# The first products of an encoder kernel issued one by one as their operands come, with the first statistics behind both groups

## The chip, the cores and the metric

One core of a Trainium2 chip runs the whole program. The metric is device time in microseconds, the median of the runs of one kernel. TensorE multiplies, VectorE and ScalarE do arithmetic and copies, GpSimd (POOL in the profile) a few additions and its own DMAs, and SyncE (SP) issues most of the DMAs.

## The reference

Two layers over 512 tokens of width 1024, in float32. Each layer is a token mixer and a squared-ReLU MLP with 4096 hidden units, each ahead of it an RMS norm and behind it a plain residual addition; a last RMS norm ends it.

```python
def rms_norm(x, g):
    y = xf * lax.rsqrt(jnp.mean(xf * xf, axis=-1, keepdims=True) + EPS)
    return (y * g.astype(jnp.float32)).astype(x.dtype)

def reference(...):
    for i in range(DEPTH):
        h = rms_norm(x, mix_norm[i])
        if i % N_MIXERS == 0:
            x = x + neighbourhood_attention(h, na_w_qkv[j], na_rpb[j], na_w_o[j])
        else:
            x = x + sliding_window_gqa(h, swa_w_qkv[j], swa_sinks[j], t5_rel_table, swa_w_o[j])
        h = rms_norm(x, mlp_norm[i])
        x = x + squared_relu_mlp(h, mlp_w_in[i], mlp_w_out[i])
    return rms_norm(x, final_norm)
```

The change lies in the first norm of layer 0 and the first three groups of its QKV projection: queries, keys and values of the first pair of heads.

## The kernel before

**Layout.** x is held transposed: 8 tiles (k = 0 to 7) of 128 features by 512 tokens. Weights come in a stream of chunks of 128x1024 (8 blocks of 128x128), through the two halves of `w_raw`. A group n is one output tile of 128x512, the sum over the 8 tiles k.

**Split precision.** Every operand is cut into a high part (a copy rounded to fp32r) and a low part (what the rounding left). A product of two operands is three matmuls, high by high, high weights by low h, low weights by high h; `part` (L654 to L656 by way of `product`) issues the three of each tile k in a row. ScalarE makes the high parts, VectorE the low ones. A chunk's high part is counted by the semaphore `w_hi_made`, its low part by `w_split`; for h the counters are `first_hi` and `h_low`.

**The norm.** h here is x times the gain, without the division by the root of the mean square, which is applied to the products at the end. ScalarE squares each tile (L1457), VectorE adds the squares into `sqsum` (`first_sum`, L1611, counter `h_split`). TensorE sums over the partitions, one column for 128 tokens (`token_statistics`, L729); ScalarE takes the root (L1124), VectorE the reciprocal (L1972), TensorE spreads the four columns back over the partitions (`spread_token_rstd`, L737), ScalarE copies them to `rstd` (L1127), and VectorE scales the groups' sums with it (`scale_tile`, L1531).

**Around the change.** Each engine runs its own list in the written order; semaphores alone tie them together. At the start TensorE runs 12 matmuls on constant data (`keep_busy`, L723), then `first_groups`: for each k, behind `h_low` k+1, the three matmuls of group 0 and, from k = 1, those of group 1 (tile 0 of group 1 between); the statistics stand ahead of group 1's last tile, the spread behind it, and then all of group 2, whose weights (the third chunk) lie in a spare place and whose sums have a bank of their own (`first_values`). Then comes `na_step(1)`, whose scores (L774) need queries and keys scaled and split (`tile_high` L1145 on ScalarE, `tile_low` L1541 on VectorE, counter `tile_split`). VectorE's list at the start is: split of chunk 0, low parts of h 0 and 1, split of chunk 1, low part 2, additions 0 and 1, then in turn a low part and an addition; behind them, the split of the third chunk (L1616), the reciprocal, scaling of groups 0 and 1, the split of the fourth chunk, the two `tile_low`, the scaling of group 2. ScalarE waits for addition k − 3 before its square k, as three squares fit in the buffer. GpSimd adds the mask to the attention bias (L563) and issues its DMAs (L552). SyncE loads a chunk when the chunk before the last has been split.

Of the kernel before, what the change touches and what calls it, by code (L numbers as in the profile page):

```python
# [22 lines left out]
P = 128  # L23
# [5 lines left out]
KT = D // P  # L29
# [132 lines left out]
def encoder(nc, xT, wstream, gains, rpb, sinks, rel_table, na_mask, onehot, out):  # L162
# [4 lines left out]
    with ExitStack() as ctx:  # L167
        def sb(name, shape, dt=F32):
            return ctx.enter_context(nc.sbuf_tensor(name, shape, dt))

        def sem(name):
            return ctx.enter_context(nc.semaphore(name))

        x = sb("x_res", [P, KT, SEQ])
        h_hi, h_lo = sb("h_hi", [P, KT, SEQ], F32R), sb("h_lo", [P, KT, SEQ], F32R)
# [6 lines left out]
        def chunk_parts(t, half):  # L182
            return w_parts[:, half, t, 0:2 * CHUNK].rearrange("p (n f) -> p n f", n=2)

        w_hi, w_lo = chunk_parts(0, 0), chunk_parts(1, 0)
# [48 lines left out]
        acc = [ctx.enter_context(nc.psum_tensor(f"acc{n}", [P, SEQ], F32)) for n in range(2)]  # L234
# [18 lines left out]
        w_hi_made, w_split, w_used = sem("w_hi_made"), sem("w_split"), sem("w_used")  # L253
# [14 lines left out]
        idle_made, h_low, first_hi = sem("idle_made"), sem("h_low"), sem("first_hi")  # L268
# [24 lines left out]
        spare_hi, spare_lo = (t[:, 0:2, :].rearrange("p a b -> p (a b)") for t in (u_hi, u_lo))  # L293
        first_values = pt_ps[:, 4:8, :].rearrange("p a b -> p (a b)")

        def f32(ap):
            return ap.bitcast(F32)
# [57 lines left out]
        def first_square(k):  # L355

            return probs[:, SEQ * (k % 3):SEQ * (k % 3 + 1)]
# [293 lines left out]
        def _(pe):  # L651
            def product(dst, a, b, start, stop, resumed=False):

                nc.tensor.matmul(dst, a[0], b[0], start=start, stop=False, skip_group_check=resumed)  # L654
                nc.tensor.matmul(dst, a[0], b[1], start=False, stop=False, skip_group_check=resumed)  # L655
                return nc.tensor.matmul(dst, a[1], b[0], start=False, stop=stop, skip_group_check=resumed)  # L656
# [7 lines left out]
            def part(c, g, tile, ks, k0=0, first=True, last=True, taken=False, bank=None, weights=None):  # L664

                hi, lo = weights or (w_hi[:, c.odd, :], w_lo[:, c.odd, :])
                bank = acc[g.odd][:] if bank is None else bank
                if ks[0] == 0:
                    pe.wait_ge(w_split, (c + 1).v)
                    if first and g.a >= 2 and not taken:  # L670
                        pe.wait_ge(acc_taken, (g + -1).v)
                for k in ks:
                    b = slice(k * P, (k + 1) * P)
                    ins = product(bank, (hi[:, b], lo[:, b]), tile(k0 + k),
                                  first and k == 0, last and k == BLOCKS - 1)
                if ks[-1] == BLOCKS - 1:
                    ins.then_inc(w_used, 1)

            ALL = range(BLOCKS)
# [45 lines left out]
            def token_statistics(n):  # L725

                pe.wait_ge(h_split, KT * (n + 1))
                for b in range(QT):
                    ins = nc.tensor.matmul(misc_ps[:, 0, b:b + 1], sqsum[:, b * P:(b + 1) * P], ones[:, 0:1],  # L729
                                           start=True, stop=True)  # L730
                ins.then_inc(stat_done, 1)

            def spread_token_rstd(n):

                pe.wait_ge(rstd_made, n + 1)
                for b in range(QT):
                    ins = nc.tensor.transpose(misc_ps[:, b, :], first_std[:, b:b + 1].to_broadcast([P, P]), ident[:])  # L737
                ins.then_inc(first_rstd_done, 1)

            def first_groups():  # L740

                for k in ALL:
                    pe.wait_ge(h_low, k + 1)
                    part(At(0), At(0), h_tile, [k])
                    if k == 1:
                        part(At(1), At(1), h_tile, [0])
                    if k == KT - 1:
                        token_statistics(0)
                    if k >= 1:
                        part(At(1), At(1), h_tile, [k])  # L750
                spread_token_rstd(0)
                part(At(2), At(2), h_tile, ALL, taken=True, bank=first_values, weights=(spare_hi, spare_lo))

            def part_after_norm(c, g, n):

# [294 lines left out]
            pe.wait_ge(filled, 1)  # L1050
            pe.wait_ge(ident_made, 1)
            first_groups()
            na_step(At(1))
            with pe.Fori(0, 3) as i:
# [444 lines left out]
        def _(dve):  # L1499
            def split_weights(c):  # L1500
                dve.wait_ge(w_hi_made, (c + 1).v)
                nc.vector.tensor_tensor(w_lo[:, c.odd, :], w_raw[:, c.odd, :], f32(w_hi[:, c.odd, :]),
                                        ALU.subtract).then_inc(w_split, 1)
# [94 lines left out]
            def first_low(k):  # L1598

                dve.wait_ge(first_hi, k + 1)  # L1600
                nc.vector.scalar_tensor_tensor(out=h_lo[:, k, :], in0=x[:, k, :], scalar=gain[:, k:k + 1],  # L1601
                                               in1=f32(h_hi[:, k, :]), op0=ALU.mult, op1=ALU.subtract).then_inc(h_low, 1)

            def first_sum(k):

                dve.wait_ge(x_prepared, k + 1)
                if k == 0:
                    dve.wait_ge(sq_cleared, 1)
                else:
                    dve.wait_ge(h_split, k)  # L1610
                nc.vector.tensor_tensor(sqsum[:], sqsum[:], first_square(k), ALU.add).then_inc(h_split, 1)  # L1611
# [480 lines left out]
            dve.wait_ge(gain_landed, 16)  # L2092
            first_low(0)
            first_low(1)
            split_weights(At(1))
            first_low(2)
            first_sum(0)
            first_sum(1)
            for k in range(3, KT):
                first_low(k)  # L2100
# [146 lines left out]
```

## Time and profile before

| | |
|---|---|
| median of 3 runs | 1098.15 us (1097.77 to 1098.61) |
| profiled execution, as timed | 1099.16 us |
| its span, first to last instruction | 1097.4 us |
| TensorE busy | 1084.2 us (99%) |
| VectorE, ScalarE, GpSimd busy | 80%, 54%, 14% |
| mean granted TensorE clock | 0.997 |

All times in the rows are microseconds from the start of the span. The timeline gives start, duration, engine, line, operation, output and inputs, shape and count; brackets give the idle time of the engine before it and what ended that. A matmul's shown duration holds its way through the array, so in a dense row the next one starts before the end of the last; the pace is read from the starts.

### The profile page before, as it was taken

The numbers are of one execution on the slowest core, as the hardware profiler recorded it, in microseconds if no ns is written. First come the engines' busy times: TensorE is split into PE (matmuls) and PEld (weight loads), VectorE is DVE, ScalarE is ACT, GpSimd is POOL, SyncE is SP. The second block draws the span as 40 slices with busy tenths as digits, with TensorE's granted clock in tenths as the row PEclk, the third lists the DMA queues.
The fourth block names the chain that finished last, engine by engine and source line by source line (L and its number), as shares of the span: only waits on it lengthen the run. The fifth ranks groups of instructions, "written<-read, shape, count | busy, mean of one in ns | idle before, by whom it ended". The sixth has DMA issues, their size and how long they took to land. (4 is left out here: it accounts for less than half of the span.)

```text
span 1097.4 us, 18105 instructions
## 1 busy us (share of the span) xinstructions
PE 1084.2 (99%) x6502; PEld 956.5 (87%) x6502; DVE 880.7 (80%) x1515; ACT 596.4 (54%) x1017; POOL 150.4 (14%) x252
## 2 busy tenths in 40 slices
PE   8999999999999999999999999999999999999997
PEld 6888888888998998898997888888899899899896
DVE  7778888678867877876996799976895895985997
ACT  6777767655425424434464788845542542642543
POOL 5555432200000000000030244200000000000000
PEclk9999999999999999999999999999999999999998
DMA  6434333333332322223242233234313323323412
GB/s 208 129 109 117 109 109 91 87 114 121 116 103 90 115 79 103 104 85 114 86 126 71 61 103 90 73 106 134 114 61 133 92 83 117 96 96 116 128 46 77
DMA packets 38361, 112.79 MB, mean 103 GB/s; under 512 B 6720, under 2 KB 11104, under 8 KB 38288
## 3 DMA queue, kind: packets, MB, share of 16 engines
q1 hardware_dynamic: 33376, 103.89, 29.3%
q0 software_dynamic: 4768, 7.90, 3.1%
q8 instruction: 47, 0.77, 0.3%
q14 instruction: 26, 0.21, 0.1%
q10 hardware_dynamic: 144, 0.02, 0.0%
HBM read 105.93 MB, written 2.70 MB: 99 GB/s over the span
## 5 line engine op out<-in xcount | busy, mean ns | idle before, releaser
L654 PE MATMUL acc<-h_hi,w_parts 128*128 128x512 f32 x736 | 290.4, 394 | 2.3 <-DVE h_lo L1601 1.4
L655 PE MATMUL acc<-h_lo,w_parts 128*128 128x512 f32 x736 | 286.7, 389 | 0.0
L656 PE MATMUL acc<-h_hi,w_parts 128*128 128x512 f32 x736 | 286.6, 389 | 0.0
L654 PEld LDWEIGHTS acc<-h_hi,w_parts 128*128 128x128 f32 x736 | 138.2, 188 | 34.4 <-issue 3.0
L656 PEld LDWEIGHTS acc<-h_hi,w_parts 128*128 128x128 f32 x736 | 138.2, 188 | 29.0
L655 PEld LDWEIGHTS acc<-h_lo,w_parts 128*128 128x128 f32 x736 | 138.3, 188 | 27.8 <-issue 0.5
L1283 ACT CAST w_parts<-w_raw 128x1024 fp32r<-128x1024 f32 x62 | 65.4, 1054 | 131.4 <-PE acc L656 107.4
L654 PE MATMUL pt_ps<-u_hi,w_parts 128*128 128x256 f32 x384 | 109.1, 284 | 0.4 <-DVE x_res L1826 0.2
L655 PE MATMUL pt_ps<-u_lo,w_parts 128*128 128x256 f32 x384 | 108.6, 283 | 0.0
L656 PE MATMUL pt_ps<-u_hi,w_parts 128*128 128x256 f32 x384 | 108.6, 283 | 0.0
L654 PE MATMUL s_ps<-u_hi,w_parts 128*128 128x256 f32 (+1 forms) x292 | 86.4, 296 | 0.0
L656 PE MATMUL s_ps<-u_hi,w_parts 128*128 128x256 f32 (+1 forms) x292 | 86.1, 295 | 0.0
L655 PE MATMUL s_ps<-u_lo,w_parts 128*128 128x256 f32 (+1 forms) x292 | 86.1, 295 | 0.0
L1304 ACT CAST w_parts<-room 128x1024 fp32r<-128x1024 f32 x32 | 33.5, 1048 | 96.0 <-DVE room L1755 96.0
L1839 DVE SCALAR_TENSOR_TENSOR room<-acc,rstd 128x512 f32<-128x512 f32 x64 | 43.9, 686 | 48.2 <-PE acc L656 48.1
L1328 ACT ACTIVATE room<-room 128x512 f32<-128x512 f32 x64 | 40.3, 630 | 76.9 <-DVE room L1839 76.9
L1775 DVE TENSOR_TENSOR w_parts<-room,w_parts 128x1024 fp32r<-128x1024 f32 x64 | 77.9, 1218 | 4.1 <-ACT w_parts L1304 4.1
L1734 DVE TENSOR_TENSOR w_parts<-w_raw,w_parts 128x1024 fp32r<-128x1024 f32 x60 | 73.1, 1219 | 9.5 <-ACT w_parts L1283 9.5
L580 POOL DMA_DIRECT2D room<-t_shifted x64 | 32.3, 507 | 348.7 <-DVE w_parts L1775 316.5
L654 PEld LDWEIGHTS pt_ps<-u_hi,w_parts 128*128 128x128 f32 x384 | 73.6, 192 | 1.0 <-issue 0.7
L1170 ACT ACTIVATE room<-room,nmax 128x256 f32<-128x256 f32 (+1 forms) x128 | 67.4, 529 | 12.0 <-DVE nmax L1581 11.8
L656 PEld LDWEIGHTS pt_ps<-u_hi,w_parts 128*128 128x128 f32 x384 | 73.7, 192 | 0.0
(208 smaller groups left out, 2488.8 us busy)
## 6 DMA issues: line engine op xcount, KB each, us to landing
w_raw<-in_wstream SPq DMA_DIRECT2D x148, 512.0 KB, 3.6
d_raw<-in_wstream SPq DMA_DIRECT2D x32, 512.0 KB, 5.3
room<-rpb_reversed POOLq DMA_DIRECT2D x64, 62.0 KB, 2.5
w_parts<-w_parts SPq DMA_DIRECT2D x16, 192.0 KB, 3.2
room<-t_shifted POOLq DMA_DIRECT2D x64, 48.0 KB, 2.2
x_res<-in_xT SPq DMA_DIRECT2D x8, 256.0 KB, 6.8
room<-inverse_sums SPq DMA_DIRECT2D x16, 128.0 KB, 3.2
out_y<-x_res SPq DMA_DIRECT2D x8, 256.0 KB, 2.5
```

Source lines behind the costliest of these rows:

```text
L580: pool.dma_start(bias[QC * a:QC * (a + 1), pair.odd, :, 0:BAND], t5_dram[:, heads, at:at + BAND]).then_inc(t5_bias_landed[pair.odd], 16)
L654: nc.tensor.matmul(dst, a[0], b[0], start=start, stop=False, skip_group_check=resumed)
L655: nc.tensor.matmul(dst, a[0], b[1], start=False, stop=False, skip_group_check=resumed)
L656: return nc.tensor.matmul(dst, a[1], b[0], start=False, stop=stop, skip_group_check=resumed)
L1170: return nc.scalar.activation(src, src, ACT.Exp, bias=nmax[:, slot, i:i + 1], scale=-1.0, accum_out=rsum[:, slot, i:i + 1])
L1283: nc.scalar.copy(chunk_parts(0, half)[:, c % 2, :], w_raw[:, c % 2, :]).then_inc(w_hi_made, 1)
L1304: nc.scalar.copy(weights_slot(q, g, 0, 5, 7), w_sums[:, 0:2 * QUAD]).then_inc(d_hi_made, 1)
L1328: nc.scalar.activation(at, at, ACT.Square).then_inc(squared, 1)
L1734: nc.vector.tensor_tensor(chunk_parts(1, half)[:, c % 2, :], w_raw[:, c % 2, :], f32(chunk_parts(0, half)[:, c % 2, :]), ALU.subtract).the ...
L1775: nc.vector.tensor_tensor(low, src, f32(high), ALU.subtract).then_inc(d_split, 1)
L1839: nc.vector.scalar_tensor_tensor(out=hidden[:, n % 4, :], in0=acc[c % 2][:], scalar=0.0, in1=rstd[:], op0=ALU.max, op1=ALU.mult).then_inc( ...
```

## The change

On TensorE `first_groups` is written out: for the first three tiles single matmuls, each behind the waits that its own two operands need (`first_term`), high parts first; then for k = 3 to 7 both groups tile by tile behind `h_low`; then the statistics; then tiles 0 to 2 of group 2; then the spread; then tiles 3 to 7 of group 2. The number of matmuls is the same. On VectorE the addition of the first squares moves from behind the third low part of h to ahead of the split of the second chunk.

```diff
--- before.py
+++ after.py
@@ -737,19 +737,47 @@
                     ins = nc.tensor.transpose(misc_ps[:, b, :], first_std[:, b:b + 1].to_broadcast([P, P]), ident[:])
                 ins.then_inc(first_rstd_done, 1)

+            def first_term(n, k, w, h):
+
+                b = slice(k * P, (k + 1) * P)
+                nc.tensor.matmul(acc[n][:], w[:, n, b], h[:, k, :], start=k == 0 and w is w_hi and h is h_hi, stop=False)
+
             def first_groups():

-                for k in ALL:
+                pe.wait_ge(w_hi_made, 1)
+                pe.wait_ge(first_hi, 1)
+                first_term(0, 0, w_hi, h_hi)
+                pe.wait_ge(w_split, 1)
+                first_term(0, 0, w_lo, h_hi)
+                pe.wait_ge(first_hi, 2)
+                first_term(0, 1, w_hi, h_hi)
+                first_term(0, 1, w_lo, h_hi)
+                pe.wait_ge(h_low, 1)
+                first_term(0, 0, w_hi, h_lo)
+                pe.wait_ge(h_low, 2)
+                first_term(0, 1, w_hi, h_lo)
+                pe.wait_ge(w_hi_made, 2)
+                for k in range(2):
+                    first_term(1, k, w_hi, h_hi)
+                    first_term(1, k, w_hi, h_lo)
+                pe.wait_ge(first_hi, 3)
+                first_term(0, 2, w_hi, h_hi)
+                first_term(0, 2, w_lo, h_hi)
+                pe.wait_ge(w_split, 2)
+                for k in range(2):
+                    first_term(1, k, w_lo, h_hi)
+                pe.wait_ge(h_low, 3)
+                first_term(0, 2, w_hi, h_lo)
+                part(At(1), At(1), h_tile, [2])
+                for k in range(3, KT):
                     pe.wait_ge(h_low, k + 1)
-                    part(At(0), At(0), h_tile, [k])
-                    if k == 1:
-                        part(At(1), At(1), h_tile, [0])
-                    if k == KT - 1:
-                        token_statistics(0)
-                    if k >= 1:
-                        part(At(1), At(1), h_tile, [k])
+                    for n in range(2):
+                        part(At(n), At(n), h_tile, [k])
+                token_statistics(0)
+                spare = dict(taken=True, bank=first_values, weights=(spare_hi, spare_lo))
+                part(At(2), At(2), h_tile, range(3), **spare)
                 spread_token_rstd(0)
-                part(At(2), At(2), h_tile, ALL, taken=True, bank=first_values, weights=(spare_hi, spare_lo))
+                part(At(2), At(2), h_tile, range(3, KT), **spare)

             def part_after_norm(c, g, n):

@@ -2092,9 +2120,9 @@
             dve.wait_ge(gain_landed, 16)
             first_low(0)
             first_low(1)
+            first_sum(0)
             split_weights(At(1))
             first_low(2)
-            first_sum(0)
             first_sum(1)
             for k in range(3, KT):
                 first_low(k)
```

## Rows read from the trace of the kernel before

**Rows 1.** The page's first part: busy us of each engine, share, instructions
```profile
PE 1084.2 (99%) x6502; PEld 956.5 (87%) x6502; DVE 880.7 (80%) x1515; ACT 596.4 (54%) x1017; POOL 150.4 (14%) x252
```

**Rows 2.** Stage table, first scores to 1080: stretch, length, busy of each engine, clock
```profile
28.34:1080.00 1051.66, 1050.90 (x6336) 929.69 (x6336) 850.09 (x1462) 574.66 (x979) 133.10 (x220) 1.00 0.32 100
```

**Rows 3.** Timeline of TensorE, start to scores: start, duration, engine, line, idle before
```profile
2.16 5.49 PE L723 MATMUL pt_ps<-w_parts 128*128 128x512 f32 x12 [2.16 <-DVE w_parts L2088]
9.01 0.47 PE L654 MATMUL acc<-h_hi,w_parts 128*128 128x512 f32 x1 [1.36 <-DVE h_lo L1601]
...
11.45 0.50 PE L654 MATMUL acc<-h_hi,w_parts 128*128 128x512 f32 x1 [0.84 <-DVE w_parts L1502]
...
20.21 0.39 PE L656 MATMUL acc<-h_hi,w_parts 128*128 128x512 f32 x1
20.64 1.05 PE L729 MATMUL om_ps<-ones,sqsum 128*128 128x1 f32 x8
21.55 0.49 PE L654 MATMUL acc<-h_hi,w_parts 128*128 128x512 f32 x1
...
22.34 0.60 PE L737 MATMUL om_ps<-ident,first_std 128*128 128x128 f32 x4
22.70 0.47 PE L654 MATMUL pt_ps<-h_hi,u_hi 128*128 128x512 f32 x1
...
28.02 0.39 PE L656 MATMUL pt_ps<-h_hi,u_lo 128*128 128x512 f32 x1
28.34 0.50 PE L774 MATMUL s_ps<-w_parts,u_hi 64*128 64x256 f32 x4
```

**Rows 4.** Timeline of VectorE and ScalarE in the first 20 us
```profile
6.55 1.23 DVE L1502 TENSOR_TENSOR w_parts<-w_raw,w_parts 128x1024 fp32r<-128x1024 f32 x1 [3.90 <-ACT w_parts L1094]
7.69 1.72 DVE L1601 SCALAR_TENSOR_TENSOR h_lo<-x_res,gain,h_hi 128x512 fp32r<-128x512 f32 x2
10.17 1.23 DVE L1502 TENSOR_TENSOR w_parts<-w_raw,w_parts 128x1024 fp32r<-128x1024 f32 x1 [0.76 <-ACT w_parts L1094]
11.31 0.75 DVE L1601 SCALAR_TENSOR_TENSOR h_lo<-x_res,gain,h_hi 128x512 fp32r<-128x512 f32 x1
11.98 1.48 DVE L1611 TENSOR_TENSOR sqsum<-sqsum,room 128x512 f32<-128x512 f32 x2
13.37 0.74 DVE L1601 SCALAR_TENSOR_TENSOR h_lo<-x_res,gain,h_hi 128x512 fp32r<-128x512 f32 x1
...
19.10 1.49 DVE L1611 TENSOR_TENSOR sqsum<-sqsum,room 128x512 f32<-128x512 f32 x2
...
7.04 0.61 ACT L1457 ACTIVATE room<-x_res 128x512 f32<-128x512 f32 x1
...
12.69 0.64 ACT L1457 ACTIVATE room<-x_res 128x512 f32<-128x512 f32 x1 [0.80 <-DVE sqsum L1611]
```

**Rows 5.** Timeline from the spread to the first scores, ScalarE and VectorE
```profile
22.98 0.59 ACT L1127 COPY rstd<-om_ps 128x512 f32<-128x512 f32 x1 [0.99 <-PE om_ps L737]
...
26.54 1.70 DVE L1541 TENSOR_TENSOR w_parts<-room,w_parts 128x512 fp32r<-128x512 f32 x1
28.45 1.23 DVE L1531 SCALAR_TENSOR_TENSOR room<-pt_ps,rstd 128x512 f32<-128x512 f32 x1 [0.21 <-PE pt_ps L656]
```

**Rows 6.** Waits in the first 60 us: engine, line, releaser, total, times, longest
```profile
PEld s_ps L774 <- DVE w_parts L1541: 0.4, 1, 0.4
```

**Rows 7.** Line 1541 up to 200 us: duration ns min, median, max; starts
```profile
L1541 DVE TENSOR_TENSOR u_lo<-room,u_hi x8: 684/1222/1227, 25.9 to 178.5; 128x512 fp32r<-128x512 f32 x8
L1541 DVE TENSOR_TENSOR w_parts<-room,w_parts x8: 1209/1224/1701, 26.5 to 181.6; 128x512 fp32r<-128x512 f32 x8
```

**Rows 8.** Timeline of TensorE, then the stage table, around the fall of the clock
```profile
1087.57 0.28 PE L656 MATMUL s_ps<-u_hi,w_parts 128*128 128x256 f32 x1
1088.79 0.58 PE L870 MATMUL acc<-pick,sqsum 128*128 128x2 f32 x4 [0.94 <-DVE sqsum L1700]
...
1089.80:1090.00 0.20, 0.01 (x1) 0.00 (x0) 0.00 (x0) 0.15 (x1) 0.00 (x0) 1.00 0.00 0
1090.00:1090.10 0.10, 0.00 (x0) 0.00 (x0) 0.00 (x0) 0.10 (x1) 0.00 (x0) 0.76 0.00 0
```

## The prediction

> **What bounds the kernel now.** I read the page's first part first. TensorE is busy 1084.2 of the 1097.4 us [rows 1]. A table by stage comes next: from the first attention scores (28.34) to 1080, TensorE idles 1051.66 − 1050.90 = 0.76 us [rows 2]. Whatever happens before 28.34 therefore matters through one thing only, the time at which those scores start. A shift of that start goes to the end of the kernel almost one to one, because there is no idle time behind it that could swallow or return it.
>
> Then the timeline of TensorE over the first 28 us [rows 3]. The reader is to see four breaks: 12 keep-busy matmuls end at 7.65 and the first product starts at 9.01 (1.36 idle, waiting for the low part of h); 0.84 idle before 11.45 (low part of the second weight chunk); the statistics at 20.64; and the scores at 28.34. Last, VectorE and ScalarE over the same time [rows 4, 5] and what the scores wait for: the last low part of L1541, on VectorE [rows 6]. The last product of group 2 starts at 28.02 and frees its slot at 28.25 [rows 3]; the low part ends at 26.54 + 1.70 = 28.24 [rows 5]. Two chains meet there within 0.1 us: TensorE's own products, and spread, copy, two scalings, a weight split and two low parts on ScalarE and VectorE. The change lengthens one and shortens the other.
>
> **The sum's own time.** It is made against the profiled execution: 1097.4 us of span, 1099.16 as timed, so 1.76 us lie around the span. The median of the runs shown is 1098.15, 1.01 below that execution. I carry the difference of the spans over to the median.
>
> **VectorE's order.** The first addition of squares moves ahead of the split of the second chunk. VectorE sits idle 0.76 us before that split, from 9.41 to 10.17, and one addition takes 0.69; its square is ready at 7.04 + 0.61 = 7.65 [rows 4]. So the addition is hidden in full and the split still ends at 11.40. Behind it, the two additions that took 1.48 us together (11.98) become one of 0.69, and everything from the fourth low part on comes 0.79 earlier. ScalarE keeps up: its 0.80 idle at 12.69 was a wait for this very addition [rows 4]. The fourth low part then runs 12.58 to 13.33 instead of from 13.37. One tile costs VectorE (19.10 − 13.37)/4.5 = 1.27 us, so the later ones end at 14.60, 15.87, 17.14 and 18.41. The last two additions (19.10, 1.48 to 1.49 us) end at 19.80 instead of 20.59. If the addition were not hidden, the split and all behind it would be at most 0.69 later; that hardly moves the sum, as it returns what it gained.
>
> **TensorE's order, products.** One matmul of 512 columns takes 0.228 us: 23 starts from 22.70 to 28.02 are 5.32 us, with 0.1 for the restart [rows 3]. Products go by parts now. The first can go at about 7.4 (behind the keep-busy ones); the second tile's low part ends at 9.41, the first's 0.7 before it, so 6 products are done at 9.8 instead of 10.61. The four of group 1 with the high weights start at 10.2, when the cast of the second chunk is done (VectorE's split is let go at 10.17), then the third tile's two, group 1's two with the low weights, and four more behind the third low part (12.06). That makes 18 products issued by 13.0; before, six plus (13.0 − 11.45)/0.228, or 13. TensorE leads by five products, 1.1 us. But it then runs dry: the fourth low part comes at 13.33. From 13.38 on, 30 products take 30 × 0.228 + 0.1 = 6.9 us, to 20.3, and each tile's six (1.37 us) take longer than VectorE's 1.27, so no further wait opens. Before, 45 of these 48 had started by 20.21 and three followed the statistics.
>
> **TensorE's order, statistics.** The squares are complete at 19.80, so the statistics start at 20.3 without a wait (before: 20.64) and take 21.55 − 20.64 = 0.91 [rows 3]. Now nine products of group 2 stand between them and the spread, where three of group 1 stood. Three took 22.34 − 21.55 = 0.79; nine take 0.79 + 6 × 0.228 = 2.16. Their weights are ready: the split of the third chunk follows the last addition and ends near 20.9. The spread starts at 20.3 + 0.91 + 2.16 = 23.4 instead of 22.34. Root and reciprocal were done at the latest 22.34 − 20.64 = 1.70 after the start of the statistics, which makes 22.0 now: the factors lie ready for 1.4 us while the spread waits in TensorE's queue.
>
> **The two chains again.** TensorE: spread 22.70 − 22.34 = 0.36, then 15 products, 3.5 us, free at 27.3: 1.0 earlier than 28.25. The other: from the start of the spread to the scores it was 28.34 − 22.34 = 6.00 us, of which the copy starts at 22.98 [rows 5], and none of it is touched by the change. 23.4 + 6.0 = 29.4. The scores start 1.04 us later than before, and TensorE idles 2.1 us ahead of them. The work behind shifts by less than TensorE does: the value scaling at 28.45 had 0.21 idle waiting for group 2 [rows 5], now there already, so VectorE is 0.8 late and gives no new stall. The DMA for the fifth chunk is issued 0.8 earlier, that for the sixth about 1 later, with its consumers equally late.
>
> **Bounds of what is not shown.** The break before the fourth tile could vanish: then the spread comes 0.35 sooner, change +0.7. The low part that ends the chain took 1.70, while the median of its kind is 1.22 [rows 7]; 0.48 less gives +0.2 together with the former. On the other side its neighbour took 0.68 where the median is 1.22 (+0.54), and GpSimd, whose times I leave where they were, may fall beside the last low part (another 0.5): +2.1. I take the middle, +1.04, since each duration is nearest to itself in the same stretch.
>
> The Trainium skill (SBUF — State Buffer, "Who interferes with whom") says that a VectorE instruction with two SBUF inputs competes with GpSimd's reads. The low parts of [rows 7] are of this kind, and 0.68 against 1.22 agrees with it. By that page the later chain meets GpSimd's next additions and ends nearer to the upper bound, +1.5 to +2.1.
>
> **Rivals.** *The clock falls.* This one is on the slower side. At the end of the kernel the dense matmuls stop at 1087.6, only eight small ones follow, and the granted clock falls between 1090.00 and 1090.10, some 2.4 us later [rows 8]. The new idle stretch is 2.1 us and holds no matmul at all. Against it: 1.36 us of idle before 9.01 left the pace untouched (six products from 9.01 to 10.61). The price: at the start, the lower of the two levels (1.2 GHz) held for the 12 keep-busy matmuls, 5.49 us or about 0.43 each instead of 0.228, so about 5 us at half pace cost 2.4. Sum 1.04 + 2.4 = +3.5: 1101.6. It decides as soon as the gap before the scores is long enough. The Trainium skill (TensorE: Matmul & The Clock Gate, "What's actually happening") has it that the throttled state is the default and activity releases it; by it the gap alone could cost this.
>
> *TensorE's lead comes through.* If the chain on VectorE were not what the scores wait for, they would start at 27.3 + 0.1: −0.95, 1097.2. For it speaks only that the two chains are level now; against it, that the spread's new place is 1.04 later and six microseconds of unchanged work hang on it.
>
> *The two cancel.* If the break at 13.0 vanishes and the last low part is short, the change is +0.2, 1098.35, nothing to be seen.
>
> **Numbers.** Forecast 70%: +1.04 ± 0.5, 1098.15 + 1.04 = 1099.2. Cancelling 13%, lead 4%, clock 13%. This kernel's measurement tells 0.2% (2.2 us) from no change. Forecast, cancelling and lead are within it but for the upper bound of the first, +2.1, and run noise (1%). So: faster 0.01, same 0.85, slower 0.14. The range takes 1097.7 (cancelling, with the 0.4 that the runs shown lie from their median) to 1101.0, which covers the +2.1 bound and part of the clock's case.
>
> **What would show it.** First product near 7.4, 18 products by 13.0, a short break, then none until the statistics at 20.3; spread at 23.4, rstd's copy at 24.0; TensorE idle about 2 us before the scores at 29.4, released by L1541's low part; idle after that unchanged. It is wrong if the scores start before 28.5, if the split of the second chunk ends later than 11.5, or if products behind 29.4 take 0.43 us each.

## The result and the profile after

The changed kernel takes 1101.45 us (median of 7 runs, 1100.96 to 1103.95), the kernel before 1098.26 (7 runs). The ratio is 1.0036, with an interval of 1.0027 to 1.0045: slower, by 3.2 us, and outside the range given. The seven times fall in two groups, four from 1100.96 to 1101.45 and three from 1103.30 to 1103.95. The profiled execution is one of the first group: span 1099.7, 1101.45 as timed.

TensorE from the statistics to the first slow products; columns as in [rows 3]:

```profile
19.64 0.95 PE L729 MATMUL om_ps<-ones,sqsum 128*128 128x1 f32 x8
...
22.60 0.60 PE L737 MATMUL om_ps<-ident,first_std 128*128 128x128 f32 x4
...
26.24 0.39 PE L656 MATMUL pt_ps<-h_hi,u_lo 128*128 128x512 f32 x1
28.99 0.50 PE L802 MATMUL s_ps<-w_parts,u_hi 64*128 64x256 f32 x4 [2.36 <-DVE w_parts L1569]
...
29.90 0.80 PE L654 MATMUL acc<-h_hi,w_parts 128*128 128x512 f32 x1
30.49 0.63 PE L655 MATMUL acc<-h_lo,w_parts 128*128 128x512 f32 x1
30.92 0.63 PE L656 MATMUL acc<-h_hi,w_parts 128*128 128x512 f32 x1
```

The spread is at 22.60, the last product of group 2 at 26.24, the scores at 28.99 with 2.36 us idle before them. Behind them, products that started 0.228 apart in the kernel before start 0.43 apart (30.49 to 30.92). The stage table over this stretch, where the last three columns are granted clock, DMA share and GB/s:

```profile
29.00:29.50 0.50, 0.50 (x8) 0.50 (x10) 0.50 (x1) 0.01 (x1) 0.50 (x2) 1.00 1.00 409
29.50:29.90 0.40, 0.40 (x9) 0.27 (x7) 0.40 (x1) 0.00 (x0) 0.40 (x2) 0.98 0.66 243
29.90:31.00 1.10, 1.10 (x5) 0.91 (x4) 0.90 (x6) 0.00 (x0) 1.00 (x2) 0.50 0.10 18
31.00:33.00 2.00, 2.00 (x6) 1.57 (x5) 1.80 (x5) 1.99 (x8) 1.26 (x1) 0.50 0.00 0
...
33.20:34.00 0.80, 0.80 (x5) 0.67 (x4) 0.10 (x1) 0.66 (x2) 0.80 (x2) 0.94 0.13 20
```

The clock falls just ahead of 29.9 (its mean is still 0.98 from 29.5 to 29.9), is 0.50 (1.2 GHz instead of 2.4) from there on, and rises near 33.3 (mean 0.94 from 33.2 to 34.0): 3.4 us at half pace. In the kernel before, a table in steps of 5 us has it at 1.00 in every step up to 1050. Behind the slow stretch the changed kernel runs as the kernel before does; the table from the scores to 1080:

```profile
28.99:1080.00 1051.01, 1050.24 (x6316) 928.69 (x6317) 847.70 (x1457) 571.58 (x976) 132.76 (x218) 1.00 0.31 99
```

0.77 us idle in 1051.01, against 0.76 in [rows 2]. No wait was added behind the scores.

Timeline of the changed kernel on ScalarE (first cast), VectorE and GpSimd, the counterpart of [rows 4] and [rows 5]:

```profile
4.75 1.05 ACT L1122 CAST w_parts<-w_raw 128x1024 fp32r<-128x1024 f32 x1 [1.96 <-DMA w_raw<-in_wstream]
...
8.61 0.68 DVE L1639 TENSOR_TENSOR sqsum<-sqsum,room 128x512 f32<-128x512 f32 x1
9.49 1.23 DVE L1530 TENSOR_TENSOR w_parts<-w_raw,w_parts 128x1024 fp32r<-128x1024 f32 x1 [0.20 <-ACT w_parts L1122]
...
19.03 1.22 DVE L1644 TENSOR_TENSOR u_lo<-w_raw,u_hi 128x1024 fp32r<-128x1024 f32 x1
...
26.19 1.22 DVE L1569 TENSOR_TENSOR u_lo<-room,u_hi 128x512 fp32r<-128x512 f32 x1
27.33 1.60 DVE L1569 TENSOR_TENSOR w_parts<-room,w_parts 128x512 fp32r<-128x512 f32 x1
...
20.36 2.81 POOL L563 TENSOR_TENSOR d_raw<-room,mask 128x256 f32<-128x256 f32 x4 [1.33 <-DMA sink<-in_sinks]
23.11 4.00 POOL L552 DMA_DIRECT2D room<-rpb_reversed  x8
27.13 3.77 POOL L563 TENSOR_TENSOR d_raw<-room,mask 128x256 f32<-128x256 f32 x4
```

The moved addition (8.61) fits ahead of the second split, which still waits 0.20 us for its cast. The two low parts of L1569 (L1541 before) take 1.22 and 1.60. For comparison the timeline of the kernel before, ScalarE's first cast and GpSimd's two sets of additions:

```profile
5.47 1.05 ACT L1094 CAST w_parts<-w_raw 128x1024 fp32r<-128x1024 f32 x1 [2.68 <-DMA w_raw<-in_wstream]
...
20.74 3.66 POOL L563 TENSOR_TENSOR d_raw<-room,mask 128x256 f32<-128x256 f32 x4 [1.36 <-DMA sink<-in_sinks]
...
28.36 2.83 POOL L563 TENSOR_TENSOR d_raw<-room,mask 128x256 f32<-128x256 f32 x4
```

GpSimd's first set took 3.66 us there and takes 2.81 now. The first chunk of weights does not land at the same time in every execution, as ScalarE's first cast shows (5.47 and 4.75), so I count from that cast. Counted so, the spread comes at 16.87 in the kernel before and 17.85 in the changed one (+0.98), the scores at 22.87 and 24.24 (+1.37). From the scores to the end of the span it is 1097.4 − 28.34 = 1069.06 and 1099.7 − 28.99 = 1070.71 (+1.65). The sum is 3.02 of the 3.2 us measured: later scores, and a stretch at half clock. (TensorE at half clock for 3.4 us loses 1.7.) The count from the cast is itself good to some 0.4 only: before_late_spread, a kernel of the experiments whose lists up to the statistics are those of the kernel before, has its statistics at 19.31 − 4.54 = 14.77 from the cast, where the kernel before has 20.64 − 5.47 = 15.17.

### The profile page after: what moved, and what is told of

Its sections match the earlier page's. It is cut to its first block and busy times, and to the rows that moved or that the text cites. A ratio compares the mean times of both kernels' runs of the same rounds, so it can differ in the third digit from the quotient of the medians.

```text
span 1099.7 us, 18105 instructions
## 1 busy us (share of the span) xinstructions
PE 1085.6 (99%) x6502; PEld 957.4 (87%) x6502; DVE 880.9 (80%) x1515; ACT 596.4 (54%) x1017; POOL 151.1 (14%) x252
## 5 line engine op out<-in xcount | busy, mean ns | idle before, releaser
L654 PEld LDWEIGHTS pt_ps<-u_hi,w_parts 128*128 128x128 f32 x384 | 73.7, 192 | 1.0 <-issue 0.7
L655 PEld LDWEIGHTS pt_ps<-u_lo,w_parts 128*128 128x128 f32 x384 | 73.7, 192 | 0.0
```

## The experiments

Each kernel ran in five rounds against the kernel before, whose medians in the three sets were 1098.15, 1098.19 and 1098.36. The second set (gpsimd_waits, gpsimd_waits_and_fill, split_behind_low_parts, vector_order_only) ran on another chip than the others, where the kernel before has the same median within 0.2. I call it a collision when an instruction of VectorE takes longer beside GpSimd's additions. The table is worked out from one profiled execution of each kernel, which need not be the one with the median time (kernel before 1099.16, spread_after_one_tile 1098.24, longer_chain 1099.35); "scores" counts from the first cast, "chain" is from the spread to the scores, "idle" TensorE's wait ahead of the scores, "low parts" the durations of the two low parts, "rest" from the scores to the end of the span.

| kernel | median us | scores | chain | idle | low parts | rest |
|---|---|---|---|---|---|---|
| before | 1098.26 | 22.87 | 6.00 | 0.1 | 0.68, 1.70 | 1069.06 |
| changed | 1101.45 | 24.24 | 6.39 | 2.36 | 1.22, 1.60 | 1070.71 |
| fill_gap | 1102.13 | 25.58 | 8.03 | 1.96 | 1.22, 3.24 | 1070.58 |
| before_late_spread | 1104.70 | 26.72 | 8.17 | 4.14 | 2.86, 1.59 | 1070.74 |
| tensor_order_only | 1104.55 | 26.68 | 8.47 | 4.44 | 2.86, 1.59 | 1070.44 |
| spread_after_one_tile | 1097.69 | 22.36 | 5.90 | 0.49 | 0.68, 1.65 | 1069.28 |
| statistics_back | 1097.96 | 21.81 | 6.00 | 0.1 | 0.68, 1.18 | 1069.63 |
| vector_order_only | 1097.96 | 22.37 | 6.02 | 0.1 | 0.68, 1.69 | 1069.01 |
| gpsimd_waits | 1098.35 | 22.90 | 5.34 | 1.30 | 0.68, 1.09 | 1069.02 |
| gpsimd_waits_and_fill | 1099.20 | 23.76 | 6.00 | none | 0.69, 1.21 | 1069.02 |
| split_behind_low_parts | 1099.56 | 22.53 | 4.97 | 0.94 + 0.70 | 0.69, 1.11 | 1070.11 |
| longer_chain | 1100.77 | 23.90 | 6.34 | 2.31 | 0.63, 1.07 | 1069.13 |
| longer_chain_and_fill | 1099.51 | 23.95 | 6.39 | 0.32 | 0.63, 1.12 | 1069.05 |
| one_tile_and_gpsimd_waits | 1097.68 | 21.63 | 5.42 | none | 0.69, 1.18 | 1069.76 |

**fill_gap.** Is the idle stretch the cause?

```diff
             first_groups()
+            keep_busy(9)
             na_step(At(1))
```

> The changed kernel with 9 keep-busy matmuls (constant data, result unused) ahead of the first scores. They take 9 x 0.228 = 2.05 us and fit in the 2.36 us that TensorE idles there. Theory A (the idle stretch lets the granted clock fall, and the slow stretch behind the scores is most of the loss): the clock stays up, products behind the scores start 0.228 apart, and 1.5 us or more of the loss go; only the later scores are left, about 1099.5. Rival B (the time is lost by the later scores and by waits behind them, the clock falls for another reason): no change, 1101.4.

Measured: 1102.13 (9 runs from 1099.45 to 1103.79), ratio 1.0021, interval 1.0005 to 1.0038. Three runs, 1099.45 to 1099.74, lie where theory A has them, with a mean granted clock of 0.997 to 0.998; the other six, from 1101.20 on, fit neither theory. The profiled execution is one of the six (1102.34, mean clock 0.996). The timeline of this kernel (TensorE, VectorE, GpSimd) and its stage table show why:

```profile
25.97 2.20 PE L723 MATMUL pt_ps<-w_parts 128*128 128x512 f32 x9
30.12 0.50 PE L802 MATMUL s_ps<-w_parts,u_hi 64*128 64x256 f32 x4 [1.96 <-DVE w_parts L1570]
...
25.68 1.22 DVE L1570 TENSOR_TENSOR u_lo<-room,u_hi 128x512 fp32r<-128x512 f32 x1
26.83 3.24 DVE L1570 TENSOR_TENSOR w_parts<-room,w_parts 128x512 fp32r<-128x512 f32 x1
...
27.02 3.65 POOL L563 TENSOR_TENSOR d_raw<-room,mask 128x256 f32<-128x256 f32 x4
```

and its stage table (stretch, busy times, then clock, DMA share, GB/s):

```profile
30.00:30.50 0.50, 0.38 (x6) 0.38 (x8) 0.50 (x2) 0.00 (x0) 0.50 (x1) 1.00 0.00 0
30.50:31.00 0.50, 0.50 (x10) 0.50 (x8) 0.50 (x1) 0.00 (x0) 0.17 (x1) 0.55 0.00 0
31.00:33.00 2.00, 2.00 (x10) 1.49 (x7) 1.43 (x8) 0.52 (x3) 0.00 (x0) 0.50 0.00 0
```

The filler ran from 25.97 to 28.17, and still TensorE idled 1.96 us and the clock fell behind it: the chain on VectorE had grown to 8.03 us, because the last low part took 3.24 us instead of 1.70. It starts at 26.83, and GpSimd's second set of additions at 27.02 lies beside it. A second cause, then, on top of the idle stretch. From 31.0 to 33.0 the clock is 0.50 as in the changed kernel.

**spread_after_one_tile, before_late_spread.** How the place of the spread alone acts.

```diff
-                part(At(2), At(2), h_tile, range(3), **spare)
+                part(At(2), At(2), h_tile, range(1), **spare)
                 spread_token_rstd(0)
-                part(At(2), At(2), h_tile, range(3, KT), **spare)
+                part(At(2), At(2), h_tile, range(1, KT), **spare)
```

> The changed kernel with the spread behind 1 tile of group 2 instead of 3. Six products, 6 x 0.228 = 1.37 us, leave the path to the scores; TensorE's idle stretch ahead of them shrinks from 2.36 to about 1.0 us. Theory A: no fall of the clock, the time drops by 1.37 plus the clock's price, to about 1098.3. Rival B: only the 1.37 go, 1100.1.

Measured: 1097.69 (11 runs, to 1098.50), ratio 0.9995, interval 0.9986 to 1.0004. Against the changed kernel 3.8 us less, where 1.37 left the path. This is theory A's forecast, and a little better. It does not tell the clock from the collision, as the earlier chain misses GpSimd's additions too (0.68 and 1.65).

```diff
+                spare = dict(taken=True, bank=first_values, weights=(spare_hi, spare_lo))
+                part(At(2), At(2), h_tile, range(3), **spare)
                 spread_token_rstd(0)
-                part(At(2), At(2), h_tile, ALL, taken=True, bank=first_values, weights=(spare_hi, spare_lo))
+                part(At(2), At(2), h_tile, range(3, KT), **spare)
```

> The kernel before with one edit: the spread stands behind 3 tiles of group 2. Nine products, 2.05 us, come onto the path to the scores (start near 30.4 instead of 28.34) and TensorE idles about 2.1 us ahead of them. Theory A: the clock falls here too, 1098.26 + 2.05 + 1.5 to 3.4 = 1101.8 to 1103.7. Rival B (the clock falls by what the first 13 us of the change do): 1100.3 with the clock up.

Measured: 1104.70 (5 runs from 1103.65), ratio 1.0064, interval 1.0050 to 1.0077. This one edit makes the kernel before slower than the whole change does, without the change's first 13 us. Its timeline on the three engines:

```profile
31.26 0.50 PE L776 MATMUL s_ps<-w_parts,u_hi 64*128 64x256 f32 x4 [4.14 <-DVE w_parts L1543]
...
25.55 1.36 DVE L1504 TENSOR_TENSOR w_parts<-w_raw,w_parts 128x1024 fp32r<-128x1024 f32 x1
26.83 2.86 DVE L1543 TENSOR_TENSOR u_lo<-room,u_hi 128x512 fp32r<-128x512 f32 x1
29.62 1.59 DVE L1543 TENSOR_TENSOR w_parts<-room,w_parts 128x512 fp32r<-128x512 f32 x1
...
27.05 3.23 POOL L563 TENSOR_TENSOR d_raw<-room,mask 128x256 f32<-128x256 f32 x4
```

Here it is the first of the two low parts, from 26.83, that meets GpSimd's additions at 27.05: 2.86 instead of 0.68 us, and 4.14 idle.

**statistics_back.** The first tiles by themselves.

```diff
-                    for n in range(2):
-                        part(At(n), At(n), h_tile, [k])
-                token_statistics(0)
-                spare = dict(taken=True, bank=first_values, weights=(spare_hi, spare_lo))
-                part(At(2), At(2), h_tile, range(3), **spare)
+                    part(At(0), At(0), h_tile, [k])
+                    if k == KT - 1:
+                        token_statistics(0)
+                    part(At(1), At(1), h_tile, [k])
                 spread_token_rstd(0)
-                part(At(2), At(2), h_tile, range(3, KT), **spare)
+                part(At(2), At(2), h_tile, ALL, taken=True, bank=first_values, weights=(spare_hi, spare_lo))
```

> The changed kernel's first tiles and VectorE order, with statistics ahead of group 1's last tile and spread right behind it, as before. Theory A: scores some 0.6 us earlier than in the kernel before, idle stretch ahead of them about 0.5 us, clock up: 1097.6. Rival C (the product-by-product start costs by itself, through restarts of TensorE): 1098.3 or more.

Measured: 1097.96 (11 runs), ratio 0.9998, interval 0.9989 to 1.0007. The product-by-product start costs nothing that shows. Its lead at the scores (21.81 against 22.87) does not arrive at the end: the rest is 0.57 longer, of which a wait for a DMA of values, 0.2, is seen. The table has the same for the two kernels with the spread behind one tile (rest 1069.28 and 1069.76). So "almost one to one", as the prediction has it, holds for scores that come later, and not in full for scores that come earlier.

**gpsimd_waits, gpsimd_waits_and_fill.** The collision taken away by a wait more on GpSimd.

```diff
             load_na_bias(At(1))
+            pool.wait_ge(tile_split, 2)
             masked_bias(At(0), 1)
```

> The changed kernel with one wait more: GpSimd begins its second set of mask additions (L563) only when both low parts of L1541 are done. Theory D (the late chain collides with GpSimd's additions on top of the idle stretch; a low part then takes up to 3.24 us instead of 1.2 to 1.7, and this makes the runs near 1103.5): no low part over 1.75 us, no run above 1102, all near 1101.0; the clock still falls, as the idle stretch stays near 2 us. Rival E (the runs near 1103.5 are a longer time at the low clock): they stay, two values about 2.5 us apart.

Measured: 1098.35 (11 runs; ten up to 1099.27, one 1100.91), ratio 1.0003, interval 0.9994 to 1.0012. One wait returns 3.1 us, the whole loss. Timeline of this kernel, TensorE, VectorE, GpSimd:

```profile
27.48 0.50 PE L803 MATMUL s_ps<-w_parts,u_hi 64*128 64x256 f32 x4 [1.30 <-DVE w_parts L1570]
...
25.73 0.68 DVE L1570 TENSOR_TENSOR u_lo<-room,u_hi 128x512 fp32r<-128x512 f32 x1
26.34 1.09 DVE L1570 TENSOR_TENSOR w_parts<-room,w_parts 128x512 fp32r<-128x512 f32 x1
...
27.51 2.82 POOL L563 TENSOR_TENSOR d_raw<-room,mask 128x256 f32<-128x256 f32 x4 [0.37 <-DVE w_parts L1570]
```

Both low parts are short, 0.68 and 1.09; the last one is shorter than in [rows 5] too (1.70). Of the 1.05 us that the wait takes off the changed kernel's chain (6.39 to 5.34), the kernel before pays 0.66 as well (6.00 to 5.34), so the wait does more than undo what the change did. I expected the idle stretch to stay near 2 us and the clock to fall; it is 1.30, and the clock stays up (rest 1069.02). Theory D is right on the low parts and on the upper group of times, and wrong on what remained: the collision had lengthened the idle stretch from 1.30 to 2.36, and with 1.30 the clock does not fall.

> The wait of GpSimd and the 9 keep-busy matmuls together. Under A and D both causes are gone and only the later scores are left: scores about 1 us later than in the kernel before at the same start of the weights, clock up, 1099.0 to 1099.6 in every run. If the clock falls or a run lies above 1101, a third cause is missing.

The edit is the wait of gpsimd_waits and the `keep_busy(9)` of fill_gap. Measured: 1099.20 (11 runs from 1099.04 to 1099.98), ratio 1.0008, interval 0.9999 to 1.0017. As expected in every run, with the scores at 28.38. It is slower than without the filler by 0.85, since nine keep-busy matmuls are longer than an idle stretch of 1.30: a filler that is not needed costs what it sticks out.

**split_behind_low_parts.** The chain shortened from the other end.

```diff
                 token_deviation(0, 1)
-                split_weights(At(3))
                 tile_high(At(0), ...)
                 tile_high(At(1), ...)
+                split_weights(At(3))
```

(and the same on VectorE, behind the two `tile_low`)

> The changed kernel with the fourth chunk's cast (ScalarE) and split (VectorE) moved behind the two high and two low parts that the scores wait for. The chain from the spread to the scores loses one split, 1.1 us, and ends before GpSimd's additions begin. Under A and D: idle stretch about 1.1 us, no fall of the clock, no collision, 1098.0 to 1098.6 in every run. If only the later scores counted: 1101.45 - 1.1 = 1100.3.

Measured: 1099.56 (11 runs from 1098.97 to 1103.30), ratio 1.0017, interval 1.0008 to 1.0026. Between the two expectations. The scores do come earlier (chain 4.97), but the products behind them need the split chunk, as the timeline of this kernel shows:

```profile
27.19 0.51 PE L802 MATMUL s_ps<-w_parts,u_hi 64*128 64x256 f32 x4 [0.94 <-DVE w_parts L1569]
...
28.87 0.50 PE L654 MATMUL acc<-h_hi,w_parts 128*128 128x512 f32 x1 [0.70 <-DVE w_parts L1530]
...
27.04 1.77 DVE L1530 TENSOR_TENSOR w_parts<-w_raw,w_parts 128x1024 fp32r<-128x1024 f32 x1
```

0.94 idle ahead of the scores and 0.70 behind them, and the split itself, 1.77 instead of 1.22, now meets GpSimd's additions. The collision was handed to the next instruction. Five of the eleven runs lie from 1100.68 on. Their mean granted clocks are 0.997, 0.998, 0.997, 0.996 and 0.994, where the six faster ones have 0.997 to 0.998: at least the slowest (1103.30) had a fall of the clock, and the three from 1100.68 to 1101.01 show none. What made those three slower stays open.

**vector_order_only, tensor_order_only.** The change cut into its two halves.

```diff
+            first_sum(0)
             split_weights(At(1))
             first_low(2)
-            first_sum(0)
             first_sum(1)
```

> The kernel before with VectorE's edit alone (first addition of squares ahead of the second split). It runs in idle time and brings the last additions 0.8 us forward, but TensorE is bound by its own products behind 11.45, so it gains at most the 0.2 us of the wait ahead of the statistics: 1098.0, no collision, no fall of the clock. If the edit delayed the split, 1098.9.

Measured: 1097.96 (11 runs), ratio 0.9998, interval 0.9989 to 1.0007. As expected; the difference of 0.2 is inside the interval. The second kernel is the changed one with this edit undone.

> The changed kernel with VectorE's list as before: the first addition of squares back behind the third low part. Low parts and additions come 0.7 us later, so TensorE waits longer ahead of the fourth tile and reaches the spread up to 0.7 later. The chain then lies deeper in GpSimd's additions: 1101.5 to 1104, more runs at the upper value than the changed kernel. If VectorE's edit had cost the time, 1098 to 1099.

Measured: 1104.55 (6 runs from 1101.48 to 1106.42), ratio 1.0057, interval 1.0045 to 1.0070. VectorE's edit is what kept the change at 3.2: without it the chain starts 0.36 later from the cast (spread at 18.21 against 17.85), and in the profiled execution, one of the faster three, the first low part again starts ahead of GpSimd's additions and takes 2.86, with 4.44 idle.

**longer_chain, longer_chain_and_fill.** The clock alone, without a collision: the changed kernel with the wait of gpsimd_waits and, in addition,

```diff
                 split_weights(At(3))
+                nc.vector.memset(sqsum[:], 0.0)
+                nc.vector.memset(room[:, 11 * SEQ:12 * SEQ], 0.0)
                 tile_low(At(TI_NA), ...)
```

> The changed kernel with GpSimd's wait, and two fills of unused memory (128x512 each) on VectorE ahead of the two low parts. They have no input, so nothing collides; they lengthen the chain, and TensorE's idle stretch ahead of the scores grows from 1.3 to about 2.2 us. This measures the clock alone. Theory A: the clock falls in most runs, 1098.35 + 0.9 for the later scores + 1.5 or more for the clock = 1100.8 or more. Without a fall: 1099.25.

Measured: 1100.77 (11 runs), ratio 1.0019, interval 1.0010 to 1.0028. Five runs lie from 1099.35 to 1100.13, with mean granted clocks of 0.997 to 0.998, and six from 1100.77 to 1101.88, with 0.995 to 0.997. The profiled one is the fastest; its clock stayed up (rest 1069.13) through an idle stretch of 2.31 us, as its timeline and stage table show:

```profile
28.47 0.50 PE L803 MATMUL s_ps<-w_parts,u_hi 64*128 64x256 f32 x4 [2.31 <-DVE w_parts L1570]
```

and its stage table (stretch, busy times, then clock, DMA share, GB/s):

```profile
28.40:30.00 1.60, 1.53 (x15) 1.31 (x16) 1.42 (x3) 0.14 (x1) 1.50 (x3) 1.00 0.78 310
30.00:34.00 4.00, 4.00 (x19) 3.32 (x18) 2.57 (x10) 3.27 (x11) 4.00 (x5) 1.00 0.13 8
```

> The same kernel with 9 keep-busy matmuls in the idle stretch. Same start of the scores as longer_chain, clock up under theory A: 1099.3 in every run. If it is as slow as longer_chain, the idle stretch is not what lets the clock fall.

Measured: 1099.51 (11 runs from 1099.24 to 1100.06), ratio 1.0012, interval 1.0003 to 1.0020. The scores start at the same time from the cast (23.95 and 23.90), and the upper group of times is gone. By the two groups and their mean clocks, then, the clock falls in about half of the executions after this idle stretch, at a price of 1.3 us in the median (1100.77 to 1099.51), and filling the stretch prevents it. No execution of the upper group was traced; that the fall is what they share rests on their times and mean clocks.

**one_tile_and_gpsimd_waits.** The candidate: the edits of spread_after_one_tile and of gpsimd_waits together.

> The candidate: spread behind 1 tile, and GpSimd's wait. In spread_after_one_tile (1097.69) the last low part took 1.65 us and TensorE idled 0.49 ahead of the scores; with 1.2 us for the low part that stretch is gone: 1097.2, some 1.0 below the kernel before. If the wait delays the second logits, 1097.7 or more.

Measured: 1097.68 (11 runs), ratio 0.9994, interval 0.9985 to 1.0003, the same as without the wait (1097.69). The idle stretch of 0.49 is gone, and a new one is there behind it, on the transfer that swaps halves of the values. From this kernel's view of TensorE's waits (line, releaser, total, times, longest):

```profile
PE om_ps L841 <- DMA w_parts<-w_parts: 0.5, 1, 0.5
```

Both one-tile kernels have the lowest medians of all, 0.5 to 0.7 below the kernel before, and their intervals reach over 1: a gain that this measurement does not tell from none.

## Why the prediction was wrong

**The early part: right.** Products by parts, addition hidden, a short break ahead of the fourth tile, no further wait until the statistics. These ran from the cast in the predicted order, and the spread came 0.98 later where 1.04 was forecast; that they agree within 0.1 is partly luck, as the count from the cast is good to some 0.4 only. TensorE ahead of VectorE, and the last low part as what the scores wait for: right too. So was the idle stretch within 0.3: 2.1 us forecast, 2.36 measured.

**The clock: the failed step.** The sum 1098.15 + 1.04 = 1099.2 gives the clock nothing; the fall stands beside it as a rival at 13%. It came true: 3.4 us at 0.50, and from the scores to the end 1.65 us more than before. That is most of the 2.25 us between 1099.2 and 1101.45. The case against it was that 1.36 us of idle at the start of the kernel had left the pace untouched. That was no evidence for a stretch of 2.1: gpsimd_waits bears 1.30 too, but the clock fell in fill_gap after 1.96, and in longer_chain, without any collision, in about half of the executions after 2.31. The rival's mechanism and place were right. Its time of 1101.6 is 0.15 from the median, but largely by two errors that cancel: the price was 1.65 us, not 2.4, and the scores were 1.37 later, not 1.04. The price of 2.4 was read from the pace of the 12 keep-busy matmuls, 5 us of half pace; the fall measured 3.4.

The Trainium skill (TensorE: Matmul & The Clock Gate, "What's actually happening") has the throttled state as the default that activity releases. The traces agree in the pace: the keep-busy matmuls at the start begin 0.43 apart and the products behind them 0.228, though the column of the granted clock reads 1.00 over both.

**The chain from the spread to the scores: a smaller term that was off.** The prediction had it as 6.0 us, "and none of it is touched by the change", and took each duration as it stood in the trace, "since each duration is nearest to itself in the same stretch". The durations belonged to a position beside GpSimd's work, and the position changed. The chain measured 6.39 in the profiled execution: the first low part 1.22 for 0.68, the last 1.60 for 1.70. This lies inside the stated bounds, which name the first low part at 1.22 (+0.54) and GpSimd beside the last one (0.5). The bounds were too small for what a collision can cost, up to 2.2 us in other kernels (2.86 for 0.68, 3.24 for 1.09), which made the chain 8.03 in fill_gap. Even the 1.70 of [rows 5] holds some: without GpSimd's next set close behind it the same low part takes 1.07 to 1.21.

**GpSimd's times: not where they were.** The prediction left them in place. From the cast, the second set moved forward by 0.5 (28.36 − 5.47 = 22.89 to 27.13 − 4.75 = 22.38), so the two moved towards each other. In the kernel before, VectorE's split of the third chunk (20.50, 1.22 us) overlaps GpSimd's first set (20.74), which takes 3.66; in the changed kernel the split ends at 20.25, the set begins at 20.36 and takes 2.81. How much of this is the change is open, because the set waits for a DMA and does not begin at the same time in every execution: in before_late_spread, with the split where the kernel before has it, the first set takes 2.93 and the second begins at 27.05 − 4.54 = 22.51.

**The Trainium skill's rule.** On the page SBUF — State Buffer, "Who interferes with whom", two-input instructions of VectorE compete with GpSimd's reads. The runs agree with the contention: low parts of 0.68 and 1.09 with GpSimd waiting, 2.86 and 3.24 beside its additions. The section also says that issue order decides who blocks. Single additions show the turns; fill_gap, the changed kernel and the kernel before:

```profile
29.07 1.60 POOL L563 TENSOR_TENSOR d_raw<-room,mask 128x256 f32<-128x256 f32 x1
27.96 1.57 POOL L563 TENSOR_TENSOR d_raw<-room,mask 128x256 f32<-128x256 f32 x1
20.74 1.58 POOL L563 TENSOR_TENSOR d_raw<-room,mask 128x256 f32<-128x256 f32 x1 [1.36 <-DMA sink<-in_sinks]
```

An addition takes 0.73 to 0.77 by itself, and one in each of these sets takes twice that. In fill_gap the low part is recorded from 26.83 to 30.07, and the three additions from 27.02, 27.71 and 28.40 run at their usual length; the fourth, from 29.07, is the long one. So the low part stood still for three additions and then ran its 1.0 us while the fourth waited. In the changed kernel the low part (27.33 to 28.93) came behind the first addition and ran beside the second: 1.60. In the kernel before it was the other way round: the split began 0.24 ahead of the first addition, kept its 1.22, and the addition waited. The last of these agrees with the page's order. The low part of fill_gap, recorded 0.2 ahead of GpSimd's set and yet held back, does not agree, unless GpSimd's additions begin to read before their recorded start, which the last section leaves open.

**The two groups of times: not settled.** The changed kernel's times fall in two groups 2.5 us apart. The longer low part (3.24 for 1.60) could make the upper one, as theory D has it. But its three runs also have mean granted clocks of 0.995, 0.994 and 0.994, against 0.996 in the four others. One stretch of 3.4 us at half clock takes 0.0015 off the mean (an estimate, 3.4/2 in 1100), so the three look as if they had spent about twice as long at the low clock, which by itself would be 1.7 of the 2.5 us. That is rival E of gpsimd_waits in part, and a longer idle stretch by the collision may be what leads to it. With GpSimd's wait the upper group is gone. No execution of the upper group was traced, so both parts are inferred.

**Shares.** Of the 3.2 us, about 1.65 are the clock and 1.37 the later scores: 0.98 for the later spread and 0.39 for the longer chain. The collision also acts on the first share: with GpSimd held back the idle stretch is 1.30 and the clock stays up, the scores are level with the kernel before (22.90 against 22.87), and the loss is gone. With the spread behind one tile it is gone too (22.36, 0.49 idle). So the late spread and the collision make the loss together. The collision is needed only for the length that it gives the idle stretch, as longer_chain loses 2.4 us without one.

## What to carry to other kernels

A duration read from a trace holds for its neighbours in time. Before moving an instruction by a microsecond, look at what the engine that it can collide with (GpSimd beside VectorE here) does where it will land, and price the duration from rows with and without that neighbour. A step that others wait for is not to be queued behind filler work: the nine products ahead of the spread saved TensorE 1 us that it then spent waiting. And an idle stretch of 2 us on TensorE can cost another 1.3 to 1.7 us by the clock. Such a term belongs in the sum, weighed over the whole range of the stretch, and a shorter gap that did no harm (1.36 us here) is no evidence against it.

## What the runs showed of the hardware that was not expected

- A low part with two inputs, 0.68 us by itself, takes 2.86 beside four additions of GpSimd, and another 3.24 for 1.09. The four additions take 3.23 to 3.92 for 2.82. The two engines take turns by whole instructions: in fill_gap the low part stood still for three additions of 0.7, then the fourth took 1.60.
- Low parts are slowed already when GpSimd's additions follow them closely in the trace: in fill_gap 1.22 for 0.68, from 25.68 to 26.90, with the set recorded from 27.02. With a wait in front of the set this does not occur (0.68 in gpsimd_waits). Whether GpSimd uses memory before its recorded start is open.
- TensorE's clock fell after idle stretches of 1.96, 2.36, 4.14 and 4.44 us, not after 0.49, 0.94 and 1.30, and after 2.31 in some executions only. It need not fall in the stretch itself: it fell 0.9 us after the work had resumed in the changed kernel (28.99), 0.4 after it in fill_gap (30.12), 1.1 after it in before_late_spread (31.26), and 0.2 ahead of it in tensor_order_only (31.26). It was low for 3.4 us in each of the four, and the time from the scores to the end grew by 1.4 to 1.7 us, whatever the length of the idle stretch.
